# A two-layer decoder trunk: the first section of the first feed-forward block staged by groups of columns of x

## The chip, the cores and the metric

The kernel runs on one core of one Trainium2 chip. The metric is the device time of one execution in microseconds. The kernel before took 964.67 us (median of 3 runs, 963.99 to 964.9).

## The reference, cut to what matters

Two layers of a decoder with 256 tokens and a width of 1024, float32. Each layer is feed-forward, mixer, feed-forward, each with a residual and a layer norm:

```python
def swiglu_ffn(x, w_in, w_out):
    gate, up = jnp.split(x @ w_in, 2, axis=-1)
    return (jax.nn.silu(gate) * up) @ w_out

for l in range(DEPTH):
    h = layer_norm(ALPHA * h + 0.5 * swiglu_ffn(h, ffn_w_in[l, 0], ffn_w_out[l, 0]), ln_g[l, 0], ln_b[l, 0])
    h = layer_norm(ALPHA * h + hybrid_mixer(h, w_in[l], w_o[l], ...), ln_g[l, 1], ln_b[l, 1])
    h = layer_norm(ALPHA * h + 0.5 * swiglu_ffn(h, ffn_w_in[l, 1], ffn_w_out[l, 1]), ln_g[l, 2], ln_b[l, 2])
```

The change touches only the very first piece of this: `x @ w_in` for the first 256 gate columns and the first 256 up columns of the first feed-forward block. `x` is 256 x 1024, `w_in` is 1024 x 5632.

## The kernel before

**Splitting.** Every float32 matrix product is made of three products of the shorter type fp32r: with a = a_hi + a_lo and w = w_hi + w_lo, it adds a_hi w_hi, a_lo w_hi and a_hi w_lo. So each piece of weights goes through three hands. SyncE issues its load into `raw`. ScalarE (ACT) copies it to `w_hi`, rounding. VectorE (DVE) subtracts and writes `w_lo`. Then TensorE (PE) multiplies. The activations go the same way: PE transposes blocks of `x` into a PSUM bank, ACT copies the bank to `xT_hi` (line 929 in the first section), DVE subtracts to `xT_lo` (line 1175).

**Units and the ring.** Weights come in units of 1 MB (128 partitions x 2048 floats) in a ring of three slots. SyncE loads unit u only when DVE has counted unit u - 3 in `lo_done` (`wait_slot`, issues at lines 334 and 342); ACT splits a unit (line 918) when it has landed and PE has let go of the slot; DVE follows (line 1158). A feed-forward block has 11 chunks of 256 hidden columns, with two units of input weights (k blocks 0 to 3, and 4 to 7, of 128 rows of `w_in` each) and one unit of output weights each.

**The first section.** For the first chunk the units 0 and 1 (and unit 2, the first half of chunk 1) are loaded in pieces of 256 KB, one k block each: `load_piece(u, k)`, line 405, 2 x 128 runs of 1 KB. `x` is loaded in four quarters, `load_x(t, h)`, line 398: token block t (128 tokens), 512 columns, 128 runs of 2 KB, 256 KB each. SyncE's queue is x(0,0), x(1,0), the four pieces of unit 0, x(0,1), x(1,1), the four pieces of unit 1, the four pieces of unit 2, then unit 3 (free when DVE has split unit 0), unit 4 (unit 1), unit 5 (unit 2).

PE's order is written out by hand in `first_pieces`: `first_T(0, 0)` (four transposes, line 442), one product of zeros, `first_T(1, 0)`, four products of zeros (line 473: bf16, into banks that are overwritten later), `piece(0, 0)` to `piece(0, 2)`, `first_T(0, 1)`, `first_T(1, 1)`, `piece(0, 3)`, `piece(1, 0)` to `piece(1, 3)`. Ahead of all stand seven products of zeros in `open_sums` and the wait for the identity matrix (`cst_loaded`, loaded from ACT's queue, line 1141). One piece is six products of 512 columns: two of `xT_hi` with `w_hi` (line 587, one for each token block), two of `xT_lo` with `w_hi` (line 589), two of `xT_hi` with `w_lo` (line 592), which add into banks 0 and 1. `first_T` fills bank 2 (token block 0) or 3 (token block 1).

ACT's order: `first_hi(0, 0)`, `first_hi(1, 0)`, the four pieces of unit 0 (line 924), piece 0 of unit 1, `first_hi(0, 1)`, `first_hi(1, 1)`, the rest of unit 1, unit 2, the two `silu` (line 957), unit 3 (line 918), unit 4, `begin_sum(0)` (line 951: the residual of token block 0 goes into two sum banks), `hidden_hi_first`, unit 5, `begin_sum(1)`. DVE's order is the same with `first_lo` (line 1175) and `piece_lo_part` (line 1168), then `gated` (line 1238), unit 3, unit 4.

**Behind the section.** PE's next work is chunk 1. `gate_up(1)` begins with `wait_unit(l, b + 2)`: it waits until DVE has counted unit 2 in `lo_done`, that is until all four pieces of unit 2 are split. Its products stand at lines 555 and 559; then come unit 3's, and then `out_product` (lines 519, 523, 527) with unit 4. Ahead of the first `out_product` PE waits for `sum_begun` to count four, the last of which are the two copies of `begin_sum(1)`, which stand behind unit 5 in ACT's order.

GpSimd (POOL) turns the counts of the x loads into `xn_ready`, waits until the last piece of unit 2 has landed, and loads the tables (line 1541, 768 KB).

Of the kernel before, what the change touches and what calls it, by code (L numbers as in the profile page):

```python
# [89 lines left out]
EARLY = P  # L90
CAUSAL = 3 * P
# [38 lines left out]
def trunk(nc, x, w_in, w_o, ffn_in, ffn_out, ln_gb, conv_wb, rows, consts, out):  # L130
    with ExitStack() as ctx:
# [3 lines left out]
        def sem(name):  # L135
            return ctx.enter_context(nc.semaphore(name))
# [147 lines left out]
        x_loaded = [sem(f"x_loaded{n}") for n in range(T * HALVES)]  # L284
# [27 lines left out]
        def _(eng):  # L312
# [82 lines left out]
            def load_x(t, h):  # L395

                cols = slice(h * BANK, (h + 1) * BANK)
                eng.dma_start(xn[:, t, cols], x[t * P:(t + 1) * P, cols]).then_inc(x_loaded[2 * t + h], 16)
# [9 lines left out]
            for u in range(2):  # L408
                load_x(0, u)
                load_x(1, u)  # L410
                for k in range(4):
                    load_piece(u, k)
# [16 lines left out]
        def _(eng):  # L429
# [46 lines left out]
            def open_sums():  # L476

                eng.wait_ge(zeros_ready, 1)  # L480
                zero_products(7).then_inc(sum_open, 1)
# [88 lines left out]
            def first_T(t, h):  # L570


                if h > 0:
                    eng.wait_ge(xT_ready, t + 1)
                eng.wait_ge(x_loaded[2 * t + h], 16)
                transposes(bank[2 + t], [xn[:, t, (4 * h + k) * P:(4 * h + k + 1) * P] for k in range(4)])\
                    .then_inc(xT_psum, 1)

            def piece(u, k):

                kk, cols = 4 * u + k, slice(k * BANK, (k + 1) * BANK)
                toks = [slice(t * P, (t + 1) * P) for t in range(T)]
                eng.wait_ge(xT_hi_done, 2 * u + 1)
                wait_piece(piece_hi, hi_done, u, k)
                for t in range(T):
                    eng.wait_ge(xT_hi_done, 2 * u + t + 1)
                    eng.matmul(bank[t][:, :], xT_hi[:, kk, toks[t]], w_hi[:, u, cols], start=kk == 0, stop=False)
                    eng.wait_ge(xT_ready, 2 * u + t + 1)
                    eng.matmul(bank[t][:, :], xT_lo[:, kk, toks[t]], w_hi[:, u, cols], start=False, stop=False)
                wait_piece(piece_lo, lo_done, u, k, RING)  # L590
                for t in range(T):
                    m = eng.matmul(bank[t][:, :], xT_hi[:, kk, toks[t]], w_lo[:, u, cols], start=False,
                                   stop=kk == KT - 1)
                    if kk == KT - 1:
                        m.then_inc(gu_done, 1)
                return m

            def first_pieces():

                first_T(0, 0)  # L600
                zero_products(1)
                first_T(1, 0)
                zero_products(4)
                for k in range(3):
                    piece(0, k)
                first_T(0, 1)
                first_T(1, 1)
                piece(0, 3).then_inc(unit_used, 1)
                for k in range(4):
                    piece(1, k)  # L610

# [298 lines left out]
        def _(eng):  # L910
# [15 lines left out]
            def first_hi(t, h):  # L926

                eng.wait_ge(xT_psum, 2 * h + t + 1)
                eng.activation(xT_hi[:, 4 * h:4 * h + 4, t * P:(t + 1) * P],
                               bank[2 + t][:, :].rearrange("p (k n) -> p k n", k=4), ACT.Copy).then_inc(xT_hi_done, 1)  # L930
# [54 lines left out]
            def ffn(l, w):  # L985
                b, f = BASE[2 * w], w * NCH
                first, last = l == w == 0, l == DEPTH - 1 and w == 1
                if first:
                    for u in range(2):
                        if u > 0:  # L990
                            piece_hi_part(u, 0)
                        first_hi(0, u)
                        first_hi(1, u)
                        if u == 0:
                            piece_hi_part(u, 0)
                        piece_hi_part(u, 1)
                        piece_hi_part(u, 2)
                        piece_hi_part(u, 3)
# [152 lines left out]
        def _(eng):  # L1151
# [19 lines left out]
            def first_lo(t, h):  # L1171

                eng.wait_ge(xT_hi_done, 2 * h + t + 1)
                part = (slice(None), slice(4 * h, 4 * h + 4), slice(t * P, (t + 1) * P))
                eng.tensor_tensor(xT_lo[part], bank[2 + t][:, :].rearrange("p (k n) -> p k n", k=4),
                                  xT_hi[part].bitcast(F32), ALU.subtract).then_inc(xT_ready, 1)
# [82 lines left out]
            def ffn(l, w):  # L1259
                b, f = BASE[2 * w], w * NCH  # L1260
                last = l == DEPTH - 1 and w == 1
                if l == w == 0:
                    for u in range(2):
                        if u > 0:
                            piece_lo_part(u, 0)
                        first_lo(0, u)
                        first_lo(1, u)
                        if u == 0:
                            piece_lo_part(u, 0)
                        piece_lo_part(u, 1)  # L1270
                        piece_lo_part(u, 2)
                        piece_lo_part(u, 3)
# [218 lines left out]
        def _(eng):  # L1491
# [43 lines left out]
            for n in range(T * HALVES):  # L1535
                eng.wait_ge(x_loaded[n], 16)
                eng.sem_inc(xn_ready, 1)
# [47 lines left out]
```

## Time and profile before

| what | value |
|---|---|
| median of 3 runs | 964.67 us (963.99 to 964.9) |
| the profiled execution | 964.01 us, of which the span of the core is 962.2 us |
| PE busy | 953.1 us, 99% of the span |
| DVE, ACT busy | 657.9 us (68%), 508.7 us (53%) |
| moved by DMA | 185.48 MB, mean 193 GB/s |
| chain that ended last | PE 94%, DVE 3%, ACT 2% |

Times in the timeline are in us from the start of the span. A timeline row reads: start, duration from the first start to the last end, engine, line, operation, output <- inputs, how many were merged, and in brackets how long the engine had been idle before and what released it. "PEld" is the weight load that goes ahead of each product, "SPq" the issue of a DMA on SyncE. In the chain of waits a row reads: start, length, engine and line.

### The profile page before, as it was taken

Reading aid. Unit: us, or ns where it says so; the run is one execution under the profiler, and the core shown is the slowest. Engines: PE = TensorE matmul, PEld = TensorE weight load, DVE = VectorE, ACT = ScalarE, POOL = GpSimd, SP = SyncE. Lnnn points to the kernel's source line nnn. Section 1 sums busy time; section 2 is a strip of 40 time slices with the busy share of each in tenths; the row PEclk is TensorE's granted clock in tenths of the full one; section 3 lists DMA queues with packets and bytes.
Section 4 is the critical chain, followed back from the end, with each engine's and each line's share of the span. In section 5 each row is a group of like instructions: output and inputs, shape, how many; then the busy total and the mean of one; then the engine's idle time right before and its main releaser. Section 6 shows DMA issues by size and latency. Waiting matters only on the chain.

```text
span 962.2 us, 14786 instructions
## 1 busy us (share of the span) xinstructions
PE 953.1 (99%) x5284; PEld 811.6 (84%) x5284; DVE 657.9 (68%) x956; ACT 508.7 (53%) x691; POOL 45.2 (5%) x51
## 2 busy tenths in 40 slices
PE   9999999999999999999999999999999999999997
PEld 6888888889878888888888888888988788888886
DVE  5656556699998555656675565667999976565565
ACT  6554545445684554455455445544557654554541
POOL 0000000011102000000010000002001010000000
PEclk9999999999999999999999999999999999999999
DMA  9766566567525656566565655565765455655551
GB/s 318 245 214 208 174 216 220 188 219 222 162 88 181 213 175 217 174 198 235 173 213 175 218 174 195 195 221 179 240 208 149 130 194 174 207 185 178 197 192 44
DMA packets 127235, 185.48 MB, mean 193 GB/s; under 512 B 6264, under 2 KB 100608, under 8 KB 126432
## 3 DMA queue, kind: packets, MB, share of 16 engines
q1 hardware_dynamic: 123584, 178.91, 56.1%
q0 software_dynamic: 3472, 6.04, 2.7%
q8 instruction: 22, 0.36, 0.2%
q14 instruction: 13, 0.11, 0.0%
q10 hardware_dynamic: 144, 0.07, 0.0%
HBM read 181.83 MB, written 1.06 MB: 190 GB/s over the span
## 4 chain that ended last, share of the span: by engine, by line
PE 94%; DVE 3%; ACT 2%; issue 0%; DVEq 0%
PE bank L555 30%; PE bank L559 16%; PE ybank L519 9%; PE ybank L527 9%; PE ybank L523 9%; PE bank L492 2%; PE bank L499 2%; PE bank L495 2%; PE ybank L775 2%; PE ybank L779 2%; PE ybank L780 2%; PE bank L442 2%; DVE w_lo L1158 1%; PE ybank L492 1%; PE ybank L495 1%; PE ybank L499 1%
## 5 line engine op out<-in xcount | busy, mean ns | idle before, releaser
L1158 DVE TENSOR_TENSOR w_lo<-raw,w_hi 128x2048 fp32r<-128x2048 f32 x154 | 352.9, 2292 | 236.2 <-ACT w_hi L918 236.2
L555 PE MATMUL bank<-xT,w_hi 128*128 128x512 f32 x1280 | 446.3, 392 | 0.0
L918 ACT ACTIVATE w_hi<-raw 128x2048 fp32r<-128x2048 f32 (+1 forms) x159 | 303.8, 1911 | 255.5 <-PE bank L559 112.1
L559 PE MATMUL bank<-xT,w_lo 128*128 128x256 f32 x1280 | 359.6, 281 | 0.0
L555 PEld LDWEIGHTS bank<-xT,w_hi 128*128 128x128 f32 x1280 | 240.2, 188 | 52.6
L559 PEld LDWEIGHTS bank<-xT,w_lo 128*128 128x128 f32 x1280 | 241.0, 188 | 1.6
L519 PE MATMUL ybank<-w_hi,yT_hi 128*128 128x512 f32 x416 | 166.0, 399 | 0.3 <-ACT ybank L951 0.3
L527 PE MATMUL ybank<-w_hi,yT_lo 128*128 128x512 f32 x416 | 163.1, 392 | 0.0
L523 PE MATMUL ybank<-w_lo,yT_hi 128*128 128x512 f32 x416 | 162.0, 389 | 0.0
L527 PEld LDWEIGHTS ybank<-w_hi,yT_lo 128*128 128x128 f32 x416 | 77.9, 187 | 19.0 <-DVE yT_lo L1475 0.7
L519 PEld LDWEIGHTS ybank<-w_hi,yT_hi 128*128 128x128 f32 x416 | 78.2, 188 | 17.1 <-issue 0.9
L523 PEld LDWEIGHTS ybank<-w_lo,yT_hi 128*128 128x128 f32 x416 | 78.2, 188 | 14.4
L971 ACT ACTIVATE gate<-gate 128x256 f32<-128x256 f32 x80 | 33.4, 418 | 53.9 <-DVE gate L1245 53.9
L964 ACT ACTIVATE gate<-bank 128x256 f32<-128x256 f32 x80 | 30.7, 384 | 51.4 <-PE bank L559 51.1
L775 PE MATMUL ybank<-xT,w_hi 128*128 128x256 f32 x192 | 55.3, 288 | 0.0
L780 PE MATMUL ybank<-xT,w_lo 128*128 128x256 f32 x192 | 54.1, 282 | 0.0
L779 PE MATMUL ybank<-xT,w_hi 128*128 128x256 f32 x192 | 54.1, 282 | 0.0
L1339 DVE SCALAR_TENSOR_TENSOR acc<-uT,cwb,acc 128x256 f32<-128x256 f32 x120 | 50.5, 479 | 0.0
L1245 DVE TENSOR_TENSOR gate<-bank,gate 128x256 f32<-128x256 f32 x80 | 33.7, 421 | 16.8 <-ACT gate L964 16.8
L1496 POOL TENSOR_TENSOR rstd<-vareps,minus_half 128x1 f32<-128x1 f32 x16 | 8.8, 552 | 738.6 <-DVE vareps L1212 679.0
L1252 DVE TENSOR_TENSOR hid<-gate,hid 128x256 f32<-128x256 f32 x80 | 34.0, 425 | 13.3 <-ACT gate L971 12.9
L492 PE MATMUL bank<-w_hi,xT 128*128 128x512 f32 (+1 forms) x112 | 41.4, 369 | 0.1
(133 smaller groups left out, 859.6 us busy)
## 6 DMA issues: line engine op xcount, KB each, us to landing
raw<-in_ffn_in SPq DMA_DIRECT2D x170, 512.0 KB, 4.6
raw<-in_ffn_out SPq DMA_DIRECT2D x88, 512.0 KB, 3.9
raw<-in_w_in SPq DMA_DIRECT2D x40, 512.0 KB, 4.5
raw<-in_w_o SPq DMA_DIRECT2D x16, 512.0 KB, 4.1
gb<-in_ln_gb SPq DMA_DIRECT2D x6, 1024.0 KB, 7.1
raw<-in_ffn_in SPq DMA_DIRECT2D x12, 256.0 KB, 6.0
raw<-in_w_in SPq DMA_DIRECT2D x4, 520.0 KB, 6.5
qk_swap<-qk_raw POOLq DMA_DIRECT2D x16, 128.0 KB, 3.0
```

Source lines behind the costliest of these rows:

```text
L492: m = eng.matmul(dst, xT_hi[:, kk, tok], wh[:, k, :], start=kk == 0, stop=False)
L519: m = eng.matmul(dst, aT_hi[:, k, tok], wh[:, k, cols], start=False, stop=False, skip_group_check=True)
L523: eng.matmul(dst, aT_hi[:, k, tok], wl[:, k, cols], start=False, stop=False, skip_group_check=True)
L527: m = eng.matmul(dst, aT_lo[:, k, tok], wh[:, k, cols], start=False, stop=ends is not None and k == 1, skip_group_check=True)
L555: m = eng.matmul(dst[:, :], wh[:, k, g, cols], xT[:, kk, :, :].rearrange("p a n -> p (a n)"), start=kk == 0, stop=False, skip_group_check= ...
L559: m = eng.matmul(dst[:, SEQ:2 * SEQ], wl[:, k, g, cols], xT_hi[:, kk, :], start=False, stop=kk == KT - 1, skip_group_check=True)
L775: e = eng.matmul(dst, wh[:, k, cols], xT_hi[:, kk, :], start=kk == 0 and m % 2 == 0, stop=False, skip_group_check=True)
L779: eng.matmul(dst, wh[:, k, cols], xT_lo[:, kk, :], start=False, stop=False, skip_group_check=True)
L780: e = eng.matmul(dst, wl[:, k, cols], xT_hi[:, kk, :], start=False, stop=kk == KT - 1, skip_group_check=True)
L918: eng.activation(w_hi[:, s, 0:width], raw[:, s, 0:width], ACT.Copy).then_inc(hi_done, 1)
L1158: eng.tensor_tensor(w_lo[:, s, 0:width], raw[:, s, 0:width], w_hi[:, s, 0:width].bitcast(F32), ALU.subtract).then_inc(lo_done, 1)
L1339: eng.scalar_tensor_tensor(acc[:, cb, :], src, w, acc[:, cb, :], ALU.mult, ALU.add)\
```

## The change

The loads of `x` are cut by columns instead of by token block: five groups of k blocks, (0), (1), (2, 3), (4, 5), (6, 7), each for both token blocks (128, 128, 256, 256, 256 KB). The first piece of weights goes ahead of x in SyncE's queue. Transposes, `first_hi` and `first_lo` go by these groups, into banks 2 and 3 by turns. PE's order becomes T0, T1, piece 0 0, T2, pieces 0 1 and 0 2, T3, pieces 0 3 and 1 0, T4, pieces 1 1 to 1 3. The products of zeros go from 7 + 1 + 4 to 6. Within a piece the two products with `xT_lo` come after the two of `xT_hi`.

```diff
+GROUPS = ((0,), (1,), (2, 3), (4, 5), (6, 7))
+GROUP_OF = {k: g for g, ks in enumerate(GROUPS) for k in ks}
...
-            def load_x(t, h):
-                cols = slice(h * BANK, (h + 1) * BANK)
-                eng.dma_start(xn[:, t, cols], x[t * P:(t + 1) * P, cols]).then_inc(x_loaded[2 * t + h], 16)
+            def load_x(g):
+                cols = slice(GROUPS[g][0] * P, (GROUPS[g][-1] + 1) * P)
+                eng.dma_start(xn[:, :, cols], x.rearrange("(t p) n -> p t n", p=P)[:, :, cols])\
+                   .then_inc(x_loaded[g], 16)
...
-            for u in range(2):
-                load_x(0, u)
-                load_x(1, u)
-                for k in range(4):
-                    load_piece(u, k)
+            load_piece(0, 0)
+            load_x(0)
+            load_x(1)
+            load_piece(0, 1)
+            load_x(2)
+            load_piece(0, 2)
+            load_piece(0, 3)
+            load_x(3)
+            load_piece(1, 0)
+            load_piece(1, 1)
+            load_x(4)
+            load_piece(1, 2)
+            load_piece(1, 3)
...
-                zero_products(7).then_inc(sum_open, 1)
+                zero_products(6).then_inc(sum_open, 1)
...
-            def first_T(t, h):
-                if h > 0:
-                    eng.wait_ge(xT_ready, t + 1)
-                eng.wait_ge(x_loaded[2 * t + h], 16)
-                transposes(bank[2 + t], [xn[:, t, (4 * h + k) * P:(4 * h + k + 1) * P] for k in range(4)])\
-                    .then_inc(xT_psum, 1)
+            def first_T(g):
+                if g > 1:
+                    eng.wait_ge(first_ready, g - 1)
+                eng.wait_ge(x_loaded[g], 16)
+                transposes(bank[2 + g % 2], [xn[:, t, k * P:(k + 1) * P] for k in GROUPS[g] for t in range(T)])\
+                    .then_inc(first_psum, 1)
...
-                eng.wait_ge(xT_hi_done, 2 * u + 1)
+                eng.wait_ge(first_hi_done, GROUP_OF[kk] + 1)
                 wait_piece(piece_hi, hi_done, u, k)
                 for t in range(T):
-                    eng.wait_ge(xT_hi_done, 2 * u + t + 1)
                     eng.matmul(bank[t][:, :], xT_hi[:, kk, toks[t]], w_hi[:, u, cols], start=kk == 0, stop=False)
-                    eng.wait_ge(xT_ready, 2 * u + t + 1)
+                eng.wait_ge(first_ready, GROUP_OF[kk] + 1)
+                for t in range(T):
                     eng.matmul(bank[t][:, :], xT_lo[:, kk, toks[t]], w_hi[:, u, cols], start=False, stop=False)
...
-                first_T(0, 0)
-                zero_products(1)
-                first_T(1, 0)
-                zero_products(4)
-                for k in range(3):
-                    piece(0, k)
-                first_T(0, 1)
-                first_T(1, 1)
+                first_T(0)
+                first_T(1)
+                piece(0, 0)
+                first_T(2)
+                piece(0, 1)
+                piece(0, 2)
+                first_T(3)
                 piece(0, 3).then_inc(unit_used, 1)
-                for k in range(4):
+                piece(1, 0)
+                first_T(4)
+                for k in range(1, 4):
                     piece(1, k)
+                eng.sem_inc(xT_psum, T * HALVES)
...
-            def first_lo(t, h):
-                eng.wait_ge(xT_hi_done, 2 * h + t + 1)
-                part = (slice(None), slice(4 * h, 4 * h + 4), slice(t * P, (t + 1) * P))
+            def first_lo(g):
+                n = len(GROUPS[g])
+                eng.wait_ge(first_hi_done, g + 1)
+                part = (slice(None), slice(GROUPS[g][0], GROUPS[g][0] + n), slice(None))
...
+                    first_lo(0)
+                    piece_lo_part(0, 0)
+                    first_lo(1)
+                    piece_lo_part(0, 1)
+                    first_lo(2)
+                    piece_lo_part(0, 2)
+                    piece_lo_part(0, 3)
+                    first_lo(3)
+                    piece_lo_part(1, 0)
+                    piece_lo_part(1, 1)
+                    first_lo(4)
+                    piece_lo_part(1, 2)
+                    piece_lo_part(1, 3)
+                    eng.sem_inc(xT_ready, T * HALVES)
                     for k in range(4):
                         piece_lo_part(2, k)
```

ACT's `first_hi` changes in the same way; its order is piece 0 0, `first_hi` 0 and 1, piece 0 1, `first_hi(2)`, pieces 0 2 and 0 3, `first_hi(3)`, pieces 1 0 and 1 1, `first_hi(4)`, pieces 1 2 and 1 3. POOL waits for all five x loads and counts `xn_ready` up by four at once.

## Rows read from the trace of the kernel before

**Rows 1.** The page: span, busy time of the engines, chain that ended last.

```profile
span 962.2 us, 14786 instructions
PE 953.1 (99%) x5284; PEld 811.6 (84%) x5284; DVE 657.9 (68%) x956; ACT 508.7 (53%) x691; POOL 45.2 (5%) x51
PE 94%; DVE 3%; ACT 2%; issue 0%; DVEq 0%
```

**Rows 2.** The timeline of the first 8 us.

```profile
0.75 0.87 SPq L398 DMA_DIRECT2D xn<-in_x  x2
1.67 2.61 SPq L405 DMA_DIRECT2D raw<-in_ffn_in  x4
...
1.57 3.17 PE L473 MATMUL ybank<-hid 128*128 128x512 bf16 x7 [1.57 <-DVE hid L1482]
2.39 0.15 PEld L473 LDWEIGHTS ybank<-hid 128*128 128x128 bf16 x1 [0.28 <-issue]
2.82 0.15 PEld L473 LDWEIGHTS ybank<-hid 128*128 128x128 bf16 x1 [0.28 <-issue]
...
4.53 0.74 PE L442 MATMUL bank<-cst,xn 128*128 128x128 f32 x4
5.30 1.25 ACT L929 ACTIVATE xT<-bank 128x512 fp32r<-128x512 f32 x2 [2.62 <-PE bank L442]
5.76 1.03 PE L473 MATMUL ybank<-hid 128*128 128x512 bf16 x4
...
7.25 0.47 PE L587 MATMUL bank<-w_hi,xT 128*128 128x512 f32 x1 [0.47 <-issue]
```

**Rows 3.** The chain of waits from 7 to 20 us.

```profile
11.63 0.87 PE bank L442 x8
...
13.44 0.46 PE bank L592 x2
...
14.83 0.46 PE bank L592 x2
```

**Rows 4.** The timeline from 11 to 20 us, the end of the first section.

```profile
11.47 1.04 PE L442 MATMUL bank<-cst,xn 128*128 128x128 f32 x8
...
12.11 1.09 ACT L929 ACTIVATE xT<-bank 128x512 fp32r<-128x512 f32 x2
12.74 1.29 DVE L1175 TENSOR_TENSOR xT<-bank,xT 128x512 fp32r<-128x512 f32 x2
13.94 4.29 DVE L1168 TENSOR_TENSOR w_lo<-raw,w_hi 128x512 fp32r<-128x512 f32 x7
...
19.31 0.40 PE L555 MATMUL bank<-xT,w_hi 128*128 128x512 f32 x1
```

**Rows 5.** The timeline from 15 to 31 us: SyncE's issues, ACT, the first out product.

```profile
15.92 0.82 SPq L342 DMA_DIRECT2D raw<-in_ffn_out  x2
...
27.66 1.92 ACT L918 ACTIVATE w_hi<-raw 128x2048 fp32r<-128x2048 f32 x1 [1.56 <-DMA raw<-in_ffn_in]
29.48 1.10 ACT L951 ACTIVATE ybank<-xn 128x512 f32<-128x512 f32 x2
...
30.90 0.39 PE L519 MATMUL ybank<-w_hi,yT_hi 128*128 128x512 f32 x1
```

**Rows 6.** Busy time by stretch; the last two columns are DMA share and GB/s.

```profile
7.00:12.00 5.00, 4.75 (x23) 3.96 (x24) 2.89 (x5) 2.68 (x5) 0.00 (x0) 1.00 1.00 329
12.00:17.00 5.00, 5.00 (x26) 4.11 (x25) 4.96 (x9) 4.79 (x9) 0.00 (x0) 1.00 1.10 368
...
22.00:27.00 5.00, 5.00 (x32) 4.45 (x31) 4.79 (x3) 3.52 (x4) 0.00 (x0) 1.00 1.00 325
```

**Rows 7.** The four quarters of x: DMA issue to landing, min/median/max.

```profile
DMA to landing us min/median/max: 3.2/4.5/5.7
```

**Rows 8.** The loads into `raw` issued in the first 12 us, likewise.

```profile
DMA to landing us min/median/max: 4.8/6.0/7.8
```

More of the change, by code:

```diff
@@ L283, in trunk @@
         y_ready = counted("y_ready", HEADS // 2)
-        x_loaded = [sem(f"x_loaded{n}") for n in range(T * HALVES)]
+        x_loaded = [sem(f"x_loaded{g}") for g in range(len(GROUPS))]
+        first_psum = sem("first_psum")
+        first_hi_done = sem("first_hi_done")
+        first_ready = sem("first_ready")
         piece_loaded = [sem(f"piece_loaded{n}") for n in range(12)]
@@ L924, in piece_hi_part, with first_hi @@
                 eng.activation(w_hi[:, u, cols], raw[:, u, cols], ACT.Copy).then_inc(piece_hi if k < 3 else hi_done, 1)
[L926 to L930, printed above, removed]
+            def first_hi(g):
+                n = len(GROUPS[g])
+                eng.wait_ge(first_psum, g + 1)
+                eng.activation(xT_hi[:, GROUPS[g][0]:GROUPS[g][0] + n, :],
+                               bank[2 + g % 2][:, 0:n * SEQ].rearrange("p (k n) -> p k n", k=n), ACT.Copy)\
+                   .then_inc(first_hi_done, 1)
             def stage_hi(l, j, tiles):
@@ L988, in ffn @@
                 if first:
[L989 to L998, printed above, removed]
+                    piece_hi_part(0, 0)
+                    first_hi(0)
+                    first_hi(1)
+                    piece_hi_part(0, 1)
+                    first_hi(2)
+                    piece_hi_part(0, 2)
+                    piece_hi_part(0, 3)
+                    first_hi(3)
+                    piece_hi_part(1, 0)
+                    piece_hi_part(1, 1)
+                    first_hi(4)
+                    piece_hi_part(1, 2)
+                    piece_hi_part(1, 3)
+                    eng.sem_inc(xT_hi_done, T * HALVES)
                     for k in range(4):
@@ L1169, in piece_lo_part @@
                    .then_inc(piece_lo if k < 3 else lo_done, 1)
-            def first_lo(t, h):
-                eng.wait_ge(xT_hi_done, 2 * h + t + 1)
-                part = (slice(None), slice(4 * h, 4 * h + 4), slice(t * P, (t + 1) * P))
-                eng.tensor_tensor(xT_lo[part], bank[2 + t][:, :].rearrange("p (k n) -> p k n", k=4),
-                                  xT_hi[part].bitcast(F32), ALU.subtract).then_inc(xT_ready, 1)
+            def first_lo(g):
+                n = len(GROUPS[g])
+                eng.wait_ge(first_hi_done, g + 1)
+                part = (slice(None), slice(GROUPS[g][0], GROUPS[g][0] + n), slice(None))
+                eng.tensor_tensor(xT_lo[part], bank[2 + g % 2][:, 0:n * SEQ].rearrange("p (k n) -> p k n", k=n),
+                                  xT_hi[part].bitcast(F32), ALU.subtract).then_inc(first_ready, 1)
             def stage_lo(l, j, t):
@@ L1262, in ffn @@
                 if l == w == 0:
[L1263 to L1272, printed above, removed]
+                    first_lo(0)
[12 more added lines that the diff above has]
+                    eng.sem_inc(xT_ready, T * HALVES)
                     for k in range(4):
@@ L1533, in _ @@
             eng.wait_ge(pool_setup, 1)
-            for n in range(T * HALVES):
-                eng.wait_ge(x_loaded[n], 16)
-                eng.sem_inc(xn_ready, 1)
+            for loaded in x_loaded:
+                eng.wait_ge(loaded, 16)
+            eng.sem_inc(xn_ready, T * HALVES)
             eng.wait_ge(cst_loaded, 16)
```

## The prediction

> **What bounds the kernel now.** I read the page first: PE is busy for 953.1 of 962.2 us and is 94% of the chain [rows 1]. The kernel is one long stretch of products, so a change in its first 20 us can be worth no more than the time by which it lets PE start earlier, if nothing behind takes that back. The timeline of the start comes next [rows 2]: PE does seven products of zeros from 1.57, transposes x from 4.53, fills the wait with more zeros and begins the first real product at 7.25. From there PE never stops. The chain shows a period of six products from 13.44 to 14.83, so 0.232 us each, and eight transposes in 0.87, so 0.109 each [rows 3]. Forty-eight products and eight transposes are 11.1 + 0.9 = 12.0 us, and 7.25 + 12.0 is the 19.31 at which chunk 1 begins [rows 4]. Last come two things that are not on the chain but close under it: DVE works without a gap from 12.74 to 18.23 [rows 4], and the DMA engines are full from 7 us on (share 1.00 to 1.10) [rows 6].
>
> What a measurement of this kernel can tell from no change is about 0.2%, 1.9 us.
>
> **Loads.** The bytes are the same. A quarter of x landed 3.2 us after its issue, one after another in SyncE's queue [rows 7]; pieces took 4.8 at best [rows 8]. A quarter costs SyncE 0.43 to issue, a piece with its 256 runs 0.65 [rows 2]. Every group of x now has 256 runs, so I take 0.65 for each. Issues: piece 0 0 at 0.75, x group 0 at 1.40, group 1 at 2.05, piece 0 1 at 2.70, group 2 at 3.35. For the landing of group 1 the bounds are 2.05 + 3.2 = 5.25 and 2.05 + 4.8 = 6.85; piece, group 0 and group 1 are together the 512 KB that the first two quarters were, and those had landed before 4.7, so I stand near the early end: 5.4. Group 2 by the same: 6.6 to 8.2. Its megabyte counted from the queue's head is what the two quarters and two pieces were (second piece issued at about 2.3 + 4.8 = 7.1), so 7.2.
>
> SyncE issues seventeen loads where it issued sixteen, five of them longer, so it reaches unit 3 about 1.3 us later than 10.97. The queue holds some 6 us of work by then [rows 8], so this costs nothing; without that backlog it would cost the 1.3.
>
> **Start of the first product.** It needs T0, T1 and ACT's copies of piece 0 0 and group 0. Group 0 lands at about 4.7; two transposes and a copy of 256 columns (a copy of 512 columns takes about 0.6 [rows 2], so 0.4) are done at 5.5. PE itself ends T1 about 0.35 after group 1 lands, so at 5.75 to 5.8. I take S = 5.8; bounds 5.5 and 7.3. That is 1.45 earlier than 7.25. ACT's copy of the piece (0.65) and DVE's two steps (0.4 + 0.7) are done 0.9 us later, as the fifth product needs them.
>
> **What PE does from there.** The eight transposes that used to come ahead of 7.25 are four now, so twelve instead of eight stand behind S: 0.44 more. PE alone would reach chunk 1 at 5.8 + 11.1 + 1.3 = 18.2, 1.1 us earlier than before. T2 is queued ahead of piece 0 1 on PE and waits for group 2: piece 0 0 ends at S + 1.4 = 7.2, which is when group 2 lands, so it costs 0, at most 1.0. T3 and T4 find their groups landed (1.8 and 2.6 MB of the queue, at 10 and 12 us, against 10.6 and 13.2).
>
> **Where it is taken back: DVE's tail.** T4 comes after five pieces and eight transposes: 5.8 + 30 x 0.232 + 8 x 0.109 = 13.6. DVE now has `first_lo(4)` ahead of pieces 1 2 and 1 3 and the four of unit 2, and nothing of these can be done earlier. The old rows give each step: from the first transpose of a bank at 11.47 to ACT at 12.11, 0.64; to DVE at 12.74, 0.63; to the next step 0.60; then seven splits in 4.29, 0.60 apart and 0.69 for the last [rows 4]. Six splits are 5 x 0.60 + 0.69 = 3.69. So unit 2 is split 0.64 + 0.63 + 0.60 + 3.69 = 5.56 after T4 begins, and PE takes up chunk 1 at 5.6 after it. PE itself has 4 x 0.109 + 18 x 0.232 = 4.6 us of work there. It stands still for 1.0 us at `wait_unit(l, b + 2)`, ahead of the first product of chunk 1, and begins it at 13.6 + 5.6 = 19.2, against 19.31. The wait for x at the front has become a wait for DVE at the end.
>
> **And under it: the load of unit 5.** Even a better order on DVE would gain little. ACT took up unit 5 at 27.66, after waiting 1.56 for its DMA; the copies of `begin_sum(1)` stand behind it, from 29.48 to 30.58; PE's first out product, which waits for them, began at 30.90 [rows 5]. So only 0.3 us separates PE from the DMA engines, which are full all the way there [rows 6] and carry the same bytes. The gain is capped at 0.3 us. SyncE frees unit 1's slot when DVE has split piece 1 3, now at 13.6 + 3.16 + 0.1 = 16.9 instead of 15.92, and unit 2's at 19.4 instead of 18.47; the engines have unit 3, then unit 4 and the tables still to move, so I put 0 on this. Its bounds are 0 and 0.9, if the queue ran dry. Runs of 512 B in groups 0 and 1 may cost the engines a little; between 0 and the whole 0.4 us that 128 more runs took to issue, I take 0.2.
>
> The counts that are passed on by PE, ACT and DVE at the section's end, and POOL's single count of four, are one instruction each; the first use of the latter is `begin_sum(0)`, some 12 us later. I cost them at nothing; if exposed, under 0.1 each.
>
> **Sum.** -0.1 for the start of chunk 1, +0.2 for the DMA engines' longer way to unit 5: +0.1. The profiled execution took 964.01, 1.8 more than its span and 0.7 less than the median; on it 964.1, on the median 964.8.
>
> **Rivals.**
> *The clock comes late (the other side).* The products of zeros are 0.43 apart at 2.39 and 2.82: 512 columns at 1.2 GHz. At 5.76 four of them take 1.03, so 0.22 apart, which is 2.4 GHz [rows 2]. PE had worked without a pause from 1.57. The granted clock column says 1.00 throughout and does not show the early part. The change takes away the fill: six products end at 4.1, then PE waits for group 0, does two transposes, waits for group 1, does two more, and starts on real work at 5.8. If the clock rises only after piece 0 1, twelve products cost 0.20 more each, 2.4, and transposes some 0.1: +2.6 in all, since T4, and with it DVE's tail, moves one for one. That gives 967.3. It decides from about ten products at the low clock. For it: three pauses instead of one. Against: PE is still busy for some 3 of the 4.2 us to 5.8. I give a late clock 0.2, most of it enough to be over 1.9.
> [...]
> *x lands late.* With group 1 at 6.9 and S at 7.3, T4 moves to 15.1 and chunk 1 to 20.7: 966.2. For it: pieces took 4.8 at best. Against: nothing else is ahead in the queue. 0.12.
> *The head start is passed on.* If DVE gets ahead of my spacing, PE keeps up to 1.1 us, cut by unit 5 to 0.3, or not cut if the load also lands earlier: 964.4 to 963.6. 0.13.
>
> **How the numbers follow.** Forecast 0.55, late clock 0.2, late x 0.12, passed on 0.13. Range: 963.6, the best end of the last rival, to 966.8, which takes in late x and the cheap half of the late clock. A loss over 1.9 needs ten slow products, or late x and a dry queue together: 0.14. A gain over 1.9 has no mechanism, since PE's whole idle and zero time to be won is below it: 0.03. Within: 0.83.
>
> **What would show it.** First real product at 5.8; group 2 waited for hardly at all; an idle of about 1.0 on PE before line 555's first weight load, released by DVE's `w_lo`, at 19.2; DVE without a gap for the 5 us ahead of it; ACT taking up unit 5 at about 27.8 behind its DMA; first out product at 31. Spacing of 0.43 in the first pieces would mean the late clock. I am wrong if chunk 1 begins before 18.8, or if the out product does before 30.6.

## The result: 969.57 us against 964.58, and the profile after

The changed kernel took 969.57 us (median of 6 runs, 967.53 to 970.54), the kernel before 964.58 (6 runs, 963.92 to 964.9). The ratio is 1.005, with an interval of 1.004 to 1.006: slower by 5.0 us, above the range that was forecast. The profiled execution took 970.54.

The page of the changed kernel, answering to [rows 1]:

```profile
span 968.7 us, 14780 instructions
PE 956.6 (99%) x5278; PEld 812.9 (84%) x5278; DVE 659.9 (68%) x957; ACT 508.7 (53%) x692; POOL 43.7 (5%) x51
PE 91%; DVE 4%; ACT 2%; DMA 1%; issue 1%; SPq 0%; DVEq 0%; ACTq 0%
```

The span grew by 6.5 and PE's busy time by 3.5, with six products fewer: some of its work ran slower. POOL, which has the same work, is busy for 1.5 less. Both are explained further down. The chain of waits through the first section shows where PE's time went first:

```profile
2.10 3.42 DMA xn<-in_x
...
5.57 0.69 PE bank L457 x2
6.25 0.85 PE bank L601 x2
...
8.81 0.85 PE bank L457 x4
9.67 0.55 PE bank L601 x2
10.22 0.46 PE bank L604 x2
```

L457 are the transposes, L601, L604 and L607 the three pairs of products of a piece. Two products take 0.85 up to 8.81, so 0.43 each, and 0.46 from 10.22, 0.23 each. The timeline has the same stretch with the start of each step:

```profile
4.51 0.66 PE L457 MATMUL bank<-cst,xn 128*128 128x128 f32 x2 [0.21 <-DMA xn<-in_x]
5.57 0.69 PE L457 MATMUL bank<-cst,xn 128*128 128x128 f32 x2 [0.39 <-DMA xn<-in_x]
5.91 1.20 PE L601 MATMUL bank<-w_hi,xT 128*128 128x512 f32 x2
...
8.61 1.05 PE L457 MATMUL bank<-cst,xn 128*128 128x128 f32 x4
...
15.82 0.60 PE L457 MATMUL bank<-cst,xn 128*128 128x128 f32 x4
...
17.09 0.69 DVE L1199 TENSOR_TENSOR xT<-bank,xT 128x512 fp32r<-128x512 f32 x1 [1.48 <-ACT xT L947]
17.69 3.69 DVE L1191 TENSOR_TENSOR w_lo<-raw,w_hi 128x512 fp32r<-128x512 f32 x6
...
21.44 0.51 PE L570 MATMUL bank<-xT,w_hi 128*128 128x512 f32 x1 [0.69 <-DVE w_lo L1191]
```

The first product began at 5.91, T2 at 8.61, T4 at 15.82, and chunk 1 at 21.44 against 19.31 in [rows 4]. Six splits took 3.69, as forecast. The five loads of x, from issue to landing (group 2 is the one of 5.1: issued at 3.20, landed at 8.34):

```profile
DMA to landing us min/median/max: 2.9/5.1/5.5
```

Up to the first out product another 0.75 is lost, answering to [rows 5]. First the chain of waits, then the timeline:

```profile
22.21 8.48 DMA raw<-in_ffn_in
...
30.72 0.04 ACT w_hi L935
...
32.54 1.11 ACT ybank L970 x2
```

```profile
30.72 1.92 ACT L935 ACTIVATE w_hi<-raw 128x2048 fp32r<-128x2048 f32 x1 [0.79 <-DMA raw<-in_ffn_in]
...
33.78 0.47 PE L534 MATMUL ybank<-w_hi,yT_hi 128*128 128x512 f32 x1 [0.48 <-ACT ybank L970]
```

This is unit 5. SyncE could issue it only when DVE had split unit 2, so from 21.62 on instead of 18.47 on; it landed at 30.69 and ACT took it up at 30.72, 3.06 later than before. The copies of `begin_sum(1)` stand behind it, and the first out product, which waits for them, is 2.88 late (33.78 for 30.90). From there on the two traces run in step until the first layer norm of the second layer, 630 us later. There, first the kernel before, then the changed one:

```profile
656.62 0.43 DVE L1252 TENSOR_TENSOR hid<-gate,hid 128x256 f32<-128x256 f32 x1 [0.22 <-ACT gate L971]
...
664.72 1.40 DVE L1225 SCALAR_TENSOR_TENSOR xn<-xn,rstd,gb 128x512 f32<-128x512 f32 x2
...
665.58 3.95 POOL L1505 TENSOR_TENSOR w_lo<-raw,w_hi 128x1024 fp32r<-128x1024 f32 x1 [1.45 <-ACT w_hi L918]
```

```profile
659.93 0.42 DVE L1276 TENSOR_TENSOR hid<-gate,hid 128x256 f32<-128x256 f32 x1 [0.60 <-ACT gate L990]
...
668.03 3.52 DVE L1249 SCALAR_TENSOR_TENSOR xn<-xn,rstd,gb 128x512 f32<-128x512 f32 x2
668.51 2.48 POOL L1533 TENSOR_TENSOR w_lo<-raw,w_hi 128x1024 fp32r<-128x1024 f32 x1 [1.07 <-ACT w_hi L935]
...
671.60 0.88 PE L457 MATMUL bank<-cst,xn 128*128 128x128 f32 x4 [1.42 <-DVE xn L1249]
```

DVE writes the normed x in two steps of 512 columns, and PE waits for each. Before, the pair took 1.40 and POOL's split of half a unit, beside it, 3.95. After, POOL's split takes 2.48 and DVE's pair 3.52: the second step lasted 2.85 instead of 0.74. That holds PE for some 2.1 us. In this profile PE's clock fell behind it too (busy time by stretch, the column before the last two is the granted clock):

```profile
670.00:675.00 5.00, 3.58 (x12) 2.82 (x12) 5.00 (x6) 2.51 (x3) 1.00 (x1) 0.69 0.20 45
```

Products there are 0.43 apart from 672.71 to 675.27, where the granted clock is 0.50 (672.7 to 675.2), and 0.23 apart from 675.52, where it is 1.00. That the first products of the section are slow by the clock is read from this same spacing. In all 3.6 us are lost here: 2.88 + 3.6 = 6.5, the growth of the span.

### The profile page after: what moved, and what is told of

The parts are those of the page before. It is cut to its first block, busy times and chain, and to the rows that moved or that the text cites. A ratio compares the mean times of both kernels' runs of the same rounds, so it can differ in the third digit from the quotient of the medians.

```text
span 968.7 us, 14780 instructions
## 1 busy us (share of the span) xinstructions
PE 956.6 (99%) x5278; PEld 812.9 (84%) x5278; DVE 659.9 (68%) x957; ACT 508.7 (53%) x692; POOL 43.7 (5%) x51
## 4 chain that ended last, share of the span: by engine, by line
PE 91%; DVE 4%; ACT 2%; DMA 1%; issue 1%; SPq 0%; DVEq 0%; ACTq 0%
PE bank L570 29%; PE bank L574 15%; PE ybank L534 9%; PE ybank L542 9%; PE ybank L538 9%; PE bank L507 3%; PE bank L510 2%; PE bank L514 2%; PE ybank L792 2%; PE ybank L796 2%; PE ybank L797 2%; PE bank L457 2%; DVE w_lo L1181 1%; ACT w_hi L935 1%; DMA raw<-in_ffn_in 1%
## 5 line engine op out<-in xcount | busy, mean ns | idle before, releaser
L1276 DVE TENSOR_TENSOR hid<-gate,hid 128x256 f32<-128x256 f32 x80 | 34.0, 425 | 13.7 <-ACT gate L990 13.6
```

## The experiments

There were fourteen runs. Milestones of their profiles, in us, all read in the same way as above. "Slow until" is the time up to which products are 0.43 and transposes 0.21 apart. It is where the trace's record of the granted clock begins; in e1, e3, e6, e8 and e11 PE stood still around that time, and only the rows on either side bear it out. The last column is DVE's second xn step in the layer norm near 668.

| kernel | slow until | first product | T2 | T4 | chunk 1 | out product | second xn step |
|---|---|---|---|---|---|---|---|
| before | 4.8 | 7.25 | | | 19.31 | 30.90 | 0.74 |
| after | 9.7 | 5.91 | 8.61 | 15.82 | 21.44 | 33.78 | 2.85 |
| e1 after again | 4.8 | 6.44 | 8.93 | 15.69 | 21.32 | 33.02 | 2.85 |
| e2 after, zeros | 5.2 | 5.67 | 8.19 | 14.98 | 20.60 | 32.29 | 2.86 |
| e3 before, few zeros | 6.4 | 7.53 | | | 19.58 | 31.17 | 0.75 |
| e4 after, POOL waits | 10.2 | 5.84 | 8.55 | 15.91 | 21.53 | 33.28 | 0.75 |
| e5 before, two rows | 6.7 | 8.11 | | | 20.18 | 31.78 | 2.85 |
| e6 after, three rows | 5.2 | 5.81 | 8.78 | 15.55 | 21.17 | 32.91 | 0.74 |
| e7 before, POOL waits | 4.7 | 7.41 | | | 19.49 | 31.08 | 0.74 |
| e8 after, mended | 5.7 | 5.93 | 8.00 | 13.20 | 19.43 | 31.12 | 0.74 |
| e9 after, T2 behind | 10.4 | 7.11 | 11.50 | 18.22 | 23.84 | 35.59 | 2.86 |
| e10 mended more | 7.3 | 6.33 | 10.10 | 15.29 | 21.51 | 33.20 | 0.75 |
| e11 e10, tables later | 6.4 | 6.97 | 10.08 | 15.27 | 21.49 | 33.19 | 0.75 |
| e12 before, tables later | 4.4 | 7.27 | | | 19.32 | 30.90 | 0.75 |
| e13 before, x by columns | 9.8 | 9.29 | | | 21.64 | 33.23 | 0.75 |
| e14 before, piece first | 5.9 | 8.10 | | | 20.14 | 31.72 | 0.75 |

**The changed kernel again.** No edit.

> The changed kernel once more, to see what repeats. The profile of it had two extra costs: the TensorE products of the first section ran 0.43 apart until 9.7 us (the first out product 2.9 us later than before), and at about 668 us one VectorE step of the layer norm took 2.9 us instead of 0.74 beside GpSimd's half of a weight split (3.6 us more). If the first is the rule and the second chance: median 967 to 970, the out product at 33 to 34.5 us in this profile too, and the long layer norm step in some profiles only, not at the same place. If the second belongs to the change: it stands at 668 us again.

Measured: 968.76 (967.46 to 969.85, 5 runs) beside 964.74 (21 runs): 1.0045, 1.0031 to 1.0059. Here PE is fast from 4.8 and chunk 1 is still 2.0 late: the late clock is no necessary part of the loss. The step of 2.85 is there again. The out product at 33.02 and the time are where they were expected if the first cost is the rule. Out product +2.12 and layer norm +2.3 are the 4.4 by which this span (966.6) is longer than that of before.

**Products of zeros put back.**

```diff
-                zero_products(6).then_inc(sum_open, 1)
+                zero_products(7).then_inc(sum_open, 1)
...
                 first_T(0)
+                zero_products(2)
                 first_T(1)
```

> The changed kernel with seven products of zeros ahead of the first transposes (instead of six) and two between the groups 0 and 1. Theory clock (the missing fill keeps TensorE at 1.2 GHz): products 0.23 apart from the first piece or its middle, chunk 1 begins at 19.2 to 19.8 as the prediction had it, the time falls by 1.5 to 3 us against the changed kernel, to 966 to 967.5. Rival (the order by groups itself costs, clock or not): the time stays within 0.7 us of the changed kernel.

Measured: 967.91 (967.57 to 968.47, 5 runs), 1.0036 (1.0022 to 1.0049). The timeline:

```profile
8.19 0.63 PE L457 MATMUL bank<-cst,xn 128*128 128x128 f32 x4 [0.76 <-DMA xn<-in_x]
...
14.98 0.60 PE L457 MATMUL bank<-cst,xn 128*128 128x128 f32 x4
```

With the fast clock from 5.2 on, PE is through with piece 0 0 at 7.4 and then waits for group 2. T2 begins 0.42 earlier than in the slow profile and T4 0.84, but 0.29 of that is group 2, which landed at 8.05 instead of 8.34. Counted from its landing, T4 comes 6.93 later here, 6.89 and 6.90 in e1 and e6, and 7.48 and 7.52 in the profiles of after and e4, which are slow until 9.7 and 10.2. So a late clock costs about 0.6 here, not 2.6: much of it lies over a wait that is there anyway. The gain of the medians over e1, 0.85, is inside the two intervals, and e1's profile was fast early too, so it is not shown that the zeros gained it. Chunk 1 came at 20.60, later than the 19.2 to 19.8 that was expected of a fast clock. The pieces show a second, smaller thing: from T2 to T4, 8.19 to 14.98, four pieces and two groups of transposes take 6.79, where 4 x 1.39 + 2 x 0.44 = 6.4 was counted. Each piece takes 1.48 to 1.55: its first product keeps PE for 0.31 instead of 0.23, and pieces 0 2 and 1 0 begin 0.07 late, just behind the end of ACT's split.

**Products of zeros taken away from the kernel before.** `zero_products(7)` becomes 6, and the ones behind `first_T(0, 0)` and `first_T(1, 0)` go.

> The kernel before with six products of zeros instead of 7 + 1 + 4, nothing else. Theory clock: the first pieces at 0.43 apart until 8 to 11 us, chunk 1 0.5 to 1.8 us later than 19.3, time 965 to 967. Rival (the fill was needless): 964.6, products 0.23 apart from 7.25 on.

Measured: 964.18 (963.84 to 965.94, 11 runs), 0.9999 (0.9989 to 1.0008). Chunk 1 0.27 later in the profile, and nothing in the medians. Removing the zeros is not what made the change slow.

**POOL held back, in the changed kernel.** Its split of half a unit waits until DVE has written the first of the four xn steps (512 columns of the first 128 tokens).

```diff
                 eng.wait_ge(hi_done, unit_count(l, u))
+                eng.wait_ge(xn_ready, count(xn_ready, l, 4 * (j + 1) + 1))
                 eng.tensor_tensor(w_lo[:, s, UNIT // 2:UNIT], raw[:, s, UNIT // 2:UNIT],
```

> The changed kernel, GpSimd starting its half of the weight split of a layer norm only when VectorE has written the first half of xn, so that it cannot come ahead of VectorE's second step. Theory race (GpSimd now and then gets there first and holds VectorE up for 2 us, TensorE stands and may drop its clock): no layer norm step over 0.8 us, the slow executions are gone, median 966.5 to 968 and a spread of under 2.5 us. Rival (the 668 us event had nothing to do with GpSimd, or hardly ever occurs): times as in the changed kernel run beside it.

Measured: 966.8 (965.67 to 967.75, 11 runs), 1.0023 (1.0014 to 1.0033), 2.0 less than e1.

```profile
659.34 0.42 DVE L1276 TENSOR_TENSOR hid<-gate,hid 128x256 f32<-128x256 f32 x1 [0.60 <-ACT gate L990]
...
667.43 1.41 DVE L1249 SCALAR_TENSOR_TENSOR xn<-xn,rstd,gb 128x512 f32<-128x512 f32 x2
...
668.33 3.92 POOL L1534 TENSOR_TENSOR w_lo<-raw,w_hi 128x1024 fp32r<-128x1024 f32 x1 [1.48 <-DVE xn L1249]
```

DVE's multiply is still late (idle 0.60 ahead of it), but now POOL starts 0.24 behind the start of DVE's second step, and it is POOL that takes 3.92. The stall is shown to be the meeting of these two instructions, and to cost 2.0.

**The same wait in the kernel before.**

> The kernel before with GpSimd waiting for the first half of xn, as in the run of the changed kernel. Theory: GpSimd is 0.2 behind VectorE there in every layer norm already, so nothing changes, 964.5 to 964.9. Rival (the wait helps any kernel): under 964.

Measured: 964.8 (963.91 to 966.49, 11 runs), 1.0002 (0.9993 to 1.0011). The wait costs nothing by itself and wins nothing where DVE is first anyway.

**Two more instructions on DVE, in the kernel before.** The first section of the change executes two more instructions on DVE, one `first_lo` and one `sem_inc`. Here two idle ones are added to the old kernel, at the start of DVE's program:

```diff
             eng.memset(uT[:, :, 0:CONV_K - 1], 0.0)
+            for _ in range(2):
+                eng.sem_inc(spare, 1)
```

> The kernel before with two more instructions in VectorE's program, ahead of everything (each counts up a semaphore that nothing reads), as many as the change adds there. In all four profiles of kernels with the changed first section VectorE starts the last multiply of hid, at about 659 us, 0.38 late, after its wait is over; in the two of kernels with the old one it does not. Theory place (a pause that belongs to a place in VectorE's program, which two added instructions move onto this multiply): the 0.38 stands at the same multiply here too, GpSimd comes 0.2 ahead of VectorE's second layer norm step near 665 us, that step takes 2.9 us, and the time is 966.5 to 967.5. Rival (the pause comes from the changed times or transfers of the first section): no pause, 964.7.

Measured: 967.12 (966.54 to 968.47, 6 runs) beside 964.38 (26 runs): 1.0031, 1.0018 to 1.0043.

```profile
657.85 0.42 DVE L1253 TENSOR_TENSOR hid<-gate,hid 128x256 f32<-128x256 f32 x1 [0.60 <-ACT gate L972]
...
665.95 3.52 DVE L1226 SCALAR_TENSOR_TENSOR xn<-xn,rstd,gb 128x512 f32<-128x512 f32 x2
666.41 2.50 POOL L1508 TENSOR_TENSOR w_lo<-raw,w_hi 128x1024 fp32r<-128x1024 f32 x1 [1.05 <-ACT w_hi L919]
```

Two instructions that do nothing, 650 us earlier, bring the whole event into the old kernel: DVE's multiply 0.38 late, POOL ahead, the long step. The rest of the 3.1 by which this span is longer is at the start: x landed at 4.60 as before, but the clock rose at 6.7 instead of 4.8, transposes and zeros ran 0.21 and 0.43 apart until then, and chunk 1 began 0.87 later.

**Three more on DVE, in the changed kernel.** The same edit with `range(3)`.

> The changed kernel with three more instructions of that kind in VectorE's program. Theory place: the pause moves three instructions ahead, onto an addition ahead of which VectorE is idle for 0.35 us anyway, the layer norm step near 668 us is 0.74 long, and the time falls by about 2, to 966.3 to 967.2. Rival: as the changed kernel, 968.8.

Measured: 966.33 (965.65 to 968.33, 9 runs), 1.0026 (1.0016 to 1.0036). It is 1.95 above the kernel before beside it, where e1 is 4.02 above its own: 2.1 less.

```profile
658.58 0.43 DVE L1277 TENSOR_TENSOR hid<-gate,hid 128x256 f32<-128x256 f32 x1 [0.22 <-ACT gate L991]
...
666.68 1.40 DVE L1250 SCALAR_TENSOR_TENSOR xn<-xn,rstd,gb 128x512 f32<-128x512 f32 x2
...
667.54 3.95 POOL L1536 TENSOR_TENSOR w_lo<-raw,w_hi 128x1024 fp32r<-128x1024 f32 x1 [1.45 <-ACT w_hi L936]
```

Adding instructions makes the changed kernel faster. The pause of 0.38 belongs to a place in DVE's program, not to its work: counted in the trace, with DVE's waits and counts of semaphores, it stands ahead of DVE's instruction 861 in all seven profiles that show it (after, e1, e2, e4, e5, e8, e9). With three more instructions 861 is another multiply, ahead of which DVE is idle for 0.35 anyway.

**The changed kernel mended.** The zeros of e2, POOL's wait of e4, and group 4 one piece earlier everywhere: `load_x(4)` ahead of `load_piece(1, 1)`, `first_T(4)` ahead of piece 1 0, `first_hi(4)` and `first_lo(4)` ahead of piece 1 1.

> The changed kernel with everything mended that the runs named so far: products of zeros as in the second run, GpSimd's wait, and group 4 of x ahead of the pieces 1 0 (TensorE) and 1 1 (loads, ScalarE, VectorE). Theory tail (chunk 1 begins 5.6 us after the transposes of group 4): these begin 1.5 us earlier with one more split behind them, chunk 1 at 19.6 to 20.0, out product 31 to 31.4, time 965 to 965.6. It would then still not be under the kernel before. Rival (the tail is not the bound): chunk 1 at 20.6 and 966 as before the mending.

Measured: 965.13 (964.56 to 967.81, 11 runs) beside 964.38: 1.001, 1.0001 to 1.0019.

```profile
8.00 0.63 PE L457 MATMUL bank<-cst,xn 128*128 128x128 f32 x4 [0.42 <-DMA xn<-in_x]
...
13.20 0.60 PE L457 MATMUL bank<-cst,xn 128*128 128x128 f32 x4
...
19.43 0.50 PE L570 MATMUL bank<-xT,w_hi 128*128 128x512 f32 x1
```

Chunk 1 follows T4 by 6.23, which is 5.62 and one more split of 0.60, and PE has no idle time left ahead of it. Of the 4.4 that e1's profile lost, 0.2 is left at the out product and 0.3 behind it, where the pause ahead of DVE's multiply still stands; the medians differ by 0.75.

**T2 behind piece 0 1, in the changed kernel.**

```diff
                 piece(0, 0)
-                first_T(2)
                 piece(0, 1)
+                first_T(2)
```

> The changed kernel with the transposes of group 2 behind piece 0 1 in TensorE's order instead of ahead of it; nothing else. In the profiles TensorE ends piece 0 0 at 7.3 to 8.5 and stands until group 2 has landed at 8.3 to 8.8. Theory (this wait is the largest cost of the first section, more than the clock): piece 0 1 fills it as soon as its weights have landed (7.7 to 8.2), the transposes of group 4 begin 0.5 to 1.2 earlier than 15.7, chunk 1 at 20.0 to 20.8, time 967.6 to 968.3. Rival (the wait is covered by others): no gain, 968.8.

Measured: 970.25 (969.79 to 971.03, 5 runs) beside 964.45 (27 runs): 1.006, 1.0046 to 1.0074.

```profile
11.50 0.60 PE L457 MATMUL bank<-cst,xn 128*128 128x128 f32 x4
...
12.13 0.60 ACT L947 ACTIVATE xT<-bank 128x512 fp32r<-128x512 f32 x1 [3.74 <-PE bank L457]
12.63 1.14 ACT L941 ACTIVATE w_hi<-raw 128x512 fp32r<-128x512 f32 x2
13.39 0.70 PE L601 MATMUL bank<-w_hi,xT 128*128 128x512 f32 x2 [1.29 <-ACT w_hi L941]
```

Worse, not better: 967.6 to 968.3 was expected. Piece 0 1 used to cover the way of T2's result from PE to ACT, and ACT does pieces 0 2 and 0 3 behind that copy. Without the cover PE stands for 1.29. The first product was late by another 1.2 in this profile, for x's second group landed later.

**The mended kernel with T2 behind piece 0 1 and three more instructions on DVE.** e8, e9's edit and e6's together.

> The mended kernel with this order too, and with three more rows in VectorE's program, which take the pause away. Theory cap: chunk 1 at 18.4 to 19.0, but the first out product still at 30.8 to 31.2, behind begin_sum(1), which waits for unit 5's load at 27.6; so 964.2 to 964.7, no better than the kernel before. Rival (the load of unit 5 comes earlier too, or isn't the bound): out product at 30.2, 963.7.

Measured: 966.3 (965.96 to 967.56, 11 runs), 1.002 (1.0011 to 1.003). Against e8 it loses 1.2 in the medians and 2.1 at chunk 1; the same idle time of 1.30 behind T2 is there. The time is 1.6 above the 964.7 and chunk 1 2.5 behind the 19.0 that were expected at most; the reason is that of e9, which ran beside it.

**The same, with the tables loaded later.** In POOL's program:

```diff
             eng.wait_ge(piece_loaded[11], 16)
+            eng.wait_ge(h_ready, 8)
             eng.dma_start(cst[:, EARLY:], consts[:, EARLY:]).then_inc(tables_loaded, 16)
```

> The same with the tables' load (768 KB, which the DMA engines move ahead of unit 5) held back until about 48 us. Theory cap: unit 5 lands 1.5 to 2 us earlier, the out product begins 0.3 to 0.7 earlier than in the run before this one, time 963.6 to 964.2, faster than the kernel before by 0.4 to 1. Rival: no difference between these two.

Measured: 966.32 (965.85 to 966.57, 11 runs), 1.0019 (1.0009 to 1.0028): no difference to e10. ACT takes up unit 5 at 28.28 instead of 29.84, and the out product is at 33.19 instead of 33.20. The load of unit 5 was not the limit, so the expected gain did not come.

**The tables later in the kernel before.**

> The kernel before with the tables' load held back in the same way, as the control: TensorE is its own bound there by 0.3 us, so the out product stays at 30.9 and the time at 964.4 to 964.8. If it falls too, the gain of the run before belongs to the tables and not to the first section.

Measured: 964.42 (963.92 to 964.81, 11 runs), 0.9999 (0.999 to 1.0008).

```profile
25.99 1.91 ACT L918 ACTIVATE w_hi<-raw 128x2048 fp32r<-128x2048 f32 x1
...
30.90 0.39 PE L519 MATMUL ybank<-w_hi,yT_hi 128*128 128x512 f32 x1
```

Unit 5 is taken up 1.67 earlier and the out product begins at the same 30.90. In the old kernel PE is its own limit there; how near the load is as a second limit no kernel was fast enough to show.

**The kernel before, the first half of x by columns.** `load_x(0, 0)` and `load_x(1, 0)` become three loads for both token blocks, with 128, 128 and 256 columns; `first_T(t, 0)` waits for all three. The order of PE, ACT and DVE is the old one.

> The kernel before, the first half of x loaded as groups 0, 1 and (2, 3) of the change (128, 128 and 256 columns of both token blocks) in place of its two quarters; transposes and all else as before, waiting for all three. Theory form (more and shorter runs delay the queue's start): the half of x lands at 5.2 to 5.8 instead of 4.6, the second piece at 7.8 to 8.4 instead of 7.2, chunk 1 0.5 to 1 later, time 965.1 to 965.7. Rival (the form costs nothing): landings within 0.3 of before, 964.5.

Measured: 966.29 (965.07 to 968.44, 11 runs) beside 964.82 (21 runs): 1.0014, 1.0005 to 1.0023.

```profile
5.67 1.08 PE L452 MATMUL bank<-cst,xn 128*128 128x128 f32 x4 [0.94 <-DMA xn<-in_x]
...
7.83 1.91 PE L483 MATMUL ybank<-hid 128*128 128x512 bf16 x4
...
9.29 0.75 PE L600 MATMUL bank<-w_hi,xT 128*128 128x512 f32 x1
```

The same bytes at the queue's head, in three loads of 256 runs instead of two of 128, landed at 5.53 instead of 4.60. The last product of zeros is slow as well (four of them in 1.91), so this profile also has the late clock. Of the 2.33 by which chunk 1 is late, 0.93 is the landing; most of the rest goes with the slow transposes and zeros. The time is above the 965.1 to 965.7 expected. The second piece of weights landed at 7.14, as before, and not at 7.8 or later.

**The kernel before, piece 0 0 ahead of x.** `load_piece(0, 0)` stands first in SyncE's queue, and nothing else changes.

> The kernel before with piece 0 0 at the head of SyncE's queue, x in quarters behind it. Theory head (the order costs, since the first bytes that TensorE can use are x): the first half of x lands at 5.2 to 5.6, the second piece at 7.2 as before since the bytes are the same, first product at 7.6 to 8.2, time 965.0 to 965.6. Rival: the piece is split while x is awaited, first product 7.0 to 7.3, 964.3 to 964.6. If the second piece lands at 8 or later here, the head of the queue is what delays the megabyte.

Measured: 965.43 (965.07 to 967.18, 11 runs), 1.0006 (0.9997 to 1.0015). The first half of x landed at 6.14, the first product came at 8.10, and the second piece landed at 7.43. The first half of x is later than the 5.2 to 5.6 expected, the rest is near it. Each of the two parts of the new queue costs the old order of work something, since that order wants all of the first half of x first. But neither alone delays the queue's first megabyte to the 8.34 that the two together show. Why they do together stays open.

## Why the prediction was wrong

**Loads: the first step that failed.** "so 7.2" for the landing of group 2. Its bounds were 6.6 and 8.2, and it landed at 8.34, and between 8.0 and 8.8 in the profiles of e1, e2, e4 and e6. I took the queue's first megabyte to land when it used to, whatever its parts; it did not. PE, which could be done with piece 0 0 at 7.2, stood still for this (0.76 in e2) or did the piece slowly meanwhile. 1.1 of T4's 2.2 is this. The rows at hand spoke for the late bound: pieces had taken 4.8 at best from their own issue, and group 2, the fifth load of the queue, was issued at 3.20, where the last load of the old megabyte was issued at 2.37. It landed 5.14 after its issue. That this is the reason is not shown, for in e13 the second piece landed 4.17 after its issue at 2.97.

**Start of the first product: right.** 5.8 forecast, 5.91 measured; 5.67 to 7.11 in the other profiles of this start, by when group 1 of x landed.

**What PE does from there: too little.** A piece was taken as six products without a gap, 1.39. It takes 1.48 to 1.55. In the new order every other piece waits a little for ACT's split, which now stands behind a `first_hi` that itself waits for PE, and the first product behind a wait or behind transposes takes 0.08 longer. From T2 to T4 that is 0.4, which I had not counted at all. T4 was put at 13.6 and came at 15.82: 1.1 for the landing, 0.1 from the landing to T2, 0.4 for these gaps, and 0.6 for the clock in this profile.

**DVE's tail: right.** 5.6 from T4 to chunk 1 was forecast. It is 5.62 in the profiles of after, e4 and e6, and 5.63 and 5.62 in e1 and e2. Since it is fixed, each tenth by which T4 is late reaches chunk 1. The idle time on PE ahead of chunk 1 was 0.69, not 1.0. Half of the difference is PE's own small waits earlier, which used up 0.16; the other half is only the way of counting, since the profile counts from the end of the last product and the sum from where the next could begin. e8 shows the other side of the same sum: T4 earlier by a piece, 6.23, and no idle time.

**The late clock: it came, and was cheap.** It is in three of the five profiles of this start (after, e4, e9; not e1, e6), so 0.2 was low for its chance. Its price of 2.6 was four times too high, for it cost 0.6: I counted every slow product in full, and the wait for group 2 covers most of them. That the clock can rise late, and that this slows the first products, was right; the term was mis-sized. The 1.2 and 2.4 GHz of the prediction are an estimate from the spacing of the zeros in the trace of before: 512 columns, taken one a period, in 0.43 from 2.39 on and in 0.21 from 5.76 on. The profiles themselves show the clock as a share, 0.50 and 1.00 around 675 in after. That work without a pause lifts the clock I took from this one change of spacing, and no run shows it. The removed products of zeros did not decide when it rose: e1, without them, is fast from 4.8, and e13, with them, slow until 9.8. They may still make a late rise rarer, which sixteen profiles do not settle: three of the six kernels with only six products of zeros are slow beyond 9 us, and one of the ten with more.

**The load of unit 5 and SyncE's slots: 0 was put on the slots.** All of DVE's tail was late, so unit 4 was issued at 19.07 instead of 15.92 [rows 5], and unit 5 at 21.62, where the sum had its slot free at 19.4. The queue did run dry: from 18 to 19 and from 19 to 20 us the DMA engines moved 210 and 221 GB/s, where they moved 396 and 401 before. ACT took up unit 5 at 30.72, not 27.8. In the profiles of e1, e2 and e6 this costs little: the out product lost 0.1 to 0.15 more than chunk 1. In the profile of after it lost 0.75 more, for unit 5 landed 8.48 after its second issue instead of 7.79 as in e1; why is not shown. The bound of 0.9 held it.

**The added instructions, put at nothing: the second step that failed.** 2.0 to 2.3 of the 5.0 come from the layer norm at 668 us, a place that the change does not touch. I costed the change's two further DVE instructions as work, one at 0.60 in DVE's tail, the other, the count, "at nothing; if exposed, under 0.1". They have a second effect, by their number: e5 brings the loss by number alone, e6 takes it away by number alone, and e4 takes it away by keeping POOL out. The condition was to be read in the old trace: DVE's second step begins 0.2 ahead of POOL's split (665.38 and 665.58), so anything that sets DVE back by more than 0.2 against ACT turns their order round.

So the sum, -0.1 and +0.2, should have been about 2.1 at the out product and 2.3 at the layer norm. That is 4.4, which is e1's span against that of before; the profile shown has 0.8 more at the out product, most of it for unit 5, and 1.3 more for the second fall of the clock. The likelier rival on the losing side named the clock, and what decided was the landing, the gaps and the layer norm. *x lands late* was nearer, but it had group 1 late and with it the first product; group 1 landed at 5.52, for 5.4, and the late one was group 2. The first two together would have been within reach of its 966.8; with the third nothing in the forecast reached 969.57.

## What to carry to other kernels

Where a first section is cut finer so that work can start earlier, add up when the last part lands and how many round trips between engines stand between two pieces: the start moved by 1.3 here, and the fixed tail behind the last group handed on every later delay. Look in the old trace for places where two engines that hold each other up start within a few tenths of each other; a change anywhere, even in the mere number of instructions, can turn their order round (e5: 967.12 beside 964.38), and one wait that fixes the order cost nothing here (e7: 964.8, a ratio of 1.0002) and guarded 2 us (e4 against e1). When a profile shows a loss far from the edit, add idle instructions to the old kernel before looking for a cause in the work.

## What the runs showed of the hardware

**A pause with a place in the program.** A multiply of 0.43 on DVE begins after 0.60 of idle time instead of 0.22 wherever it is DVE's instruction 861 (after, e1, e2, e4, e5, e8, e9), and not where it is 859 (before, e3, e7, e12 to e14) or 864 (e6, e10, e11); idle instructions far ahead move it. What the pause is stays open.

**DVE and POOL held each other up.** With POOL 0.17 ahead (after), DVE's step of 0.74 took 2.85 and ended 0.55 behind POOL's, which took 2.48. With DVE 0.20 ahead (before), POOL's took 3.95. POOL's 1.47 more is near the 1.68 from its start to the end of DVE's next split (667.26), which follows the second step without a gap. By what the two hold each other up is not shown. Who is first is not always to be read from the starts: in the profile of e14, another layer norm went the other way, with the starts as far apart as in the kernel before. First the kernel before, then e14:

```profile
295.25 3.80 POOL L1505 TENSOR_TENSOR w_lo<-raw,w_hi 128x1024 fp32r<-128x1024 f32 x1 [1.63 <-ACT w_hi L918]
295.54 1.22 DVE L1195 TENSOR_TENSOR w_lo<-raw,w_hi 128x1024 fp32r<-128x1024 f32 x1
```

```profile
296.04 2.63 POOL L1506 TENSOR_TENSOR w_lo<-raw,w_hi 128x1024 fp32r<-128x1024 f32 x1 [1.63 <-ACT w_hi L919]
296.33 3.42 DVE L1196 TENSOR_TENSOR w_lo<-raw,w_hi 128x1024 fp32r<-128x1024 f32 x1
```

Both pairs start 0.29 apart. Before, DVE's split ran through in 1.22 and POOL's was stretched; in e14 DVE's took 3.42. This meeting is in both kernels and falls either way. It may be what lies behind the single runs of the unchanged kernel at 965.8 to 966.8 in that comparison (6 of 21); that was not tested.

**No version beat the kernel before.** The best, e8, is 0.75 above it, e3 and e12 equal it. An earlier first product is worth nothing here as long as group 2 lands at 8 us and DVE's whole tail follows T4.
